# The first expert layer reordered: round 0 between the shared gate-ups, loads that wait for a gather, the shared down-projection in halves

## The reference

```python
scores = sigmoid(h @ router_w);  idx = top_k(scores + bias, 8)        # 64 experts, 8 for each token
gates  = s_sel / sum(s_sel) * 2.5
y_e    = (silu(xb @ w_gate[e]) * (xb @ w_up[e])) @ w_down[e]          # w_gate, w_up: 1024x256, w_down: 256x1024
shared = (silu(h @ sh_gate) * (h @ sh_up)) @ sh_down                  # one more expert that sees every token
x      = x + g_f * (sum over a token's experts of gate * y_e + shared)
```

## The time before, and how its profile is read

| what | value |
|---|---|
| median of three runs | 1809.76 us (1802.72, 1809.76, 1810.55) |
| the profiled execution: its own time | 1802.14 us |
| its span, first to last instruction | 1800.4 us |
| PE busy | 1642.2 us, 91% |
| DVE, ACT, POOL busy | 32%, 17%, 11% |
| data moved | 563.94 MB, mean 313 GB/s |
| mean granted TensorE clock | 0.974 |

### The profile page before, as it was taken

How to read it: one execution, slowest core, us unless ns; L and a number is a source line. 1 busy time by engine, 2 the same in 40 slices (tenths; PEclk the granted TensorE clock), 3 DMA queues, 4 the chain that set the end, 5 groups by cost and what they waited for, 6 DMA issues and landing times. The chain is left out here.

```text
span 1800.4 us, 23106 instructions
## 1 busy us (share of the span) xinstructions
PE 1642.2 (91%) x8503; PEld 725.1 (40%) x8503; DVE 580.2 (32%) x1357; ACT 298.7 (17%) x679; POOL 206.4 (11%) x197
## 2 busy tenths in 40 slices
PE   4999998999999898999998599989799899798897
PEld 2544444554333333434333244454333233233232
DVE  3131775464221122222121552375322122112122
ACT  2002443130111111111111121173100000000001
POOL 0300442001111111111110000030100000000000
PEclk9999999999999999999999799999899899999899
DMA  9613983066999999999999952303999999999995
GB/s 347 186 59 132 354 315 113 20 260 241 420 400 406 420 415 404 403 408 400 416 412 403 359 215 81 106 1 106 394 408 387 419 418 414 419 418 419 416 411 206
DMA packets 127841, 563.94 MB, mean 313 GB/s; under 512 B 17802, under 2 KB 23385, under 8 KB 78192
## 3 DMA queue, kind: packets, MB, share of 16 engines
q1 hardware_dynamic: 109344, 515.40, 71.8%
q0 software_dynamic: 17248, 43.62, 6.4%
q10 hardware_dynamic: 1136, 3.43, 0.5%
HBM read 553.10 MB, written 26.83 MB: 322 GB/s over the span
## 5 line engine op out<-in xcount | busy, mean ns | idle before, releaser
L1861 PE MATMUL ps<-wb,pool 128*32 128x512 f32 (+2 forms) x2608 | 493.0, 606 | 21.9 <-issue 21.8
L1861 PEld LDWEIGHTS ps<-wb,pool 128*32 128x32 f32 (+2 forms) x2608 | 160.2, 125 | 310.9 <-issue 310.9
L1875 DVE TENSOR_TENSOR ffn_hid<-ffn_sg,ps 128x256 f32<-128x256 f32 x71 | 29.9, 421 | 567.5 <-ACT ffn_sg L1869 567.5
L1905 PE MATMUL ps<-pool,ffn_hidT 128*32 128x512 f32 (+2 forms) x584 | 164.1, 597 | 3.5 <-DVE ffn_hidT L1890 2.3
L1905 PE MATMUL ps<-hT,ffn_hidT 128*32 128x512 f32 (+2 forms) x680 | 158.2, 603 | 5.0 <-DVE ffn_hidT L1890 3.2
L1762 POOL DMA_INDIRECT pool<-h_rows,ffn_index x71 | 73.5, 1036 | 613.6 <-DVE ffn_index L1812 318.5
L2579 PE MATMUL ps<-wb,hT 128*128 128x512 f32 x320 | 139.7, 597 | 3.0 <-issue 1.6
L1869 ACT ACTIVATE ffn_sg<-ps 128x256 f32<-128x256 f32 x71 | 27.2, 383 | 571.1 <-PE ps L1861 571.1
L1932 PE MATMUL ps<-x_res,rw 128*128 128x512 f32 x224 | 114.1, 613 | 0.9 <-DVE x_res L1944 0.9
L1905 PE MATMUL ps<-sh_wd,ffn_hidT 128*32 128x512 f32 (+2 forms) x272 | 100.1, 596 | 2.3 <-DVE ffn_hidT L1890 1.5
L1825 PE MATMUL ps<-const,pool 128*128 128x128 f32 x568 | 91.0, 284 | 10.0 <-DMA pool<-h_rows,ffn_index 7.9
(11 more groups left out here) (336 smaller groups left out, 1751.4 us busy)
## 6 DMA issues: line engine op xcount, KB each, us to landing
wb<-in_expert_w_gate_dram SPq DMA_DIRECT2D x106, 1024.0 KB, 13.1
wb<-in_expert_w_up_dram SPq DMA_DIRECT2D x106, 1024.0 KB, 19.0
pool<-in_expert_w_down_dram SPq DMA_DIRECT2D x52, 1024.0 KB, 19.9
hT<-in_expert_w_down_dram SPq DMA_DIRECT2D x52, 1024.0 KB, 17.9
wb<-in_ada_w_dram SPq DMA_DIRECT2D x24, 2048.0 KB, 10.7
sh_wd<-in_expert_w_down_dram SPq DMA_DIRECT2D x24, 1024.0 KB, 19.0
wb<-in_diff_w_in_dram SPq DMA_DIRECT2D x6, 2048.0 KB, 17.5
mix_yr<-y_rows SPq DMA_DIRECT2D x6, 2048.0 KB, 15.5
```

The lines of the kernel that those rows point to most:

```text
L1861: mm = nc.tensor.matmul(core.ps[lo:lo + width, gu_bank(n), :], xT[:, n % 2, k, lo:lo + width], w[:, k], start=k == 0, stop=k == KD - 1, sk ...
L1875: nc.vector.tensor_tensor(hid[:, n % 2, :], sg[:, n % 2, :], core.ps[:, gu_bank(n), F:2 * F], ALU.mult).then_inc(hid_ready, 1)
L1905: mm = nc.tensor.matmul(core.ps[lo:lo + width, down_bank(half), :], hidT[:, n % 2, k, lo:lo + width], wd_at(q % DR, half, k), start=k == 0 ...
```

## The change

In layer 0 only (`last` is False). The helper functions take new positions (`pos_shared`, `pos_round`), since shared tiles and rounds now share the semaphores and the two buffers of gate-up sums in the order shared 0, 1, 2, round 0, shared 3, round 1, ...

1. PE does the placing product at once and not after the second shared gate-up; the shared gate-ups 1 and 2 are cut in halves around `pe_info(0)` and `pe_turn(0)`; round 0's gate-up stands between shared gate-up 2 and 3, and `pe_info(1)` and round 0's down before round 1.
2. SP issues gate-up 0 and 1, then waits until the first gather has landed, then gate-up 2, 3, down 0, 1, gate-up 4, 5, down 2 to 5, and from 6 on gate-up q, down q. Down loads 0 to 11 use a ring of four slots, since `sh_wd` is still in use; from 12 on the ring has five.
3. The shared down-projection is cut in eight halves, each 512 columns of one tile (2 products), two in each of rounds 1 to 4, through PSUM bank 7, each followed by two DVE operations on 512 columns.
4. In every round both transposes of the next round (half 1 first) stand before `pe_turn_hidden(n)`; and for rounds from 6 on (`HEAD_ROUNDS`) one chunk of k of the next round's gate-up (`EARLY_CHUNK` = 4) stands between `pe_turn_hidden(n)` and down n. With it the wait for the next round's gate-up weights moves ahead of down n.

```diff
+        X_HALVES = (0, 1) if last else (1, 0)
+        HEAD_ROUNDS = 6
+        EARLY_CHUNK = KD // 2
+        def chunks_early(n):
+            return () if last or n < HEAD_ROUNDS else (EARLY_CHUNK,)
+        def pos_shared(i):
+            return i if last else (0, 1, 2, 4)[i]
+        def pos_round(n):
+            return n if last else 3 if n == 0 else n + 4
+        D_FOURS = 0 if last else 12
+            s = q % DR if last else q % 4 if q < D_FOURS else (q - D_FOURS - 1) % DR
...
+        def pe_shared_half(pe, j):
+            i, half = j // 2, j % 2
+            if j == 0:
+                pe.wait_ge(wd_in, 16)
+                pe.wait_ge(sums_used, 1)
+            else:
+                pe.wait_ge(sh_scaled, j)
+            pe.wait_ge(sh_hidT, pos_shared(i) + 1)
+            pe.wait_ge(index_ready, 3 if j >= 6 else 2)
+            for k in range(KF):
+                mm = nc.tensor.matmul(core.ps[:, 7, :], sh_hidden[i][:, k, :], sw.wd[:, k, half * 512:(half + 1) * 512],
+                                      start=k == 0, stop=k == KF - 1)
+            mm.then_inc(sh_down, 1)
+        def dve_shared_half(dve, j):
...
+            nc.vector.tensor_tensor(sh_prod[:, j % 2, :], core.ps[:, 7, :], r.ffn_gate[...], ALU.mult).then_inc(sh_scaled, 1)
+            dve.wait_ge(sh_scaled, j + 1)
+            nc.vector.tensor_tensor(core.x[:, t, cols], core.x[:, t, cols], sh_prod[:, j % 2, :], ALU.add).then_inc(sh_added, 1)
...
+                    for q in range(2):
+                        sp_gate_up(sp, q)
+                    sp.wait_ge(gathered[0], 16)
+                    for q in range(2, 4):
+                        sp_gate_up(sp, q)
+                    for q in range(2):
+                        sp_down(sp, q)
+                    over = overflow(sp)
+                    for q in range(4, 6):
+                        sp_gate_up(sp, q)
+                    for q in range(2, 6):
+                        sp_down(sp, q)
+                    for q in range(6, E):
+                        sp_gate_up(sp, q)
+                        if q < E - 2:
+                            sp_down(sp, q)
...
+                    dve_shared_hidden(dve, 0)
+                    dve_info(dve, 0, link)
+                    dve_shared_hidden(dve, 1)
+                    dve_shared_take(dve, 0)
...
+                    dve_take_x(dve, 0)
+                    dve_shared_take(dve, 1)
+                    dve_shared_hidden(dve, 2)
+                    dve_hidden(dve, 0)
+                    dve_hot(dve, 1)
+                    dve_shared_take(dve, 2)
+                    dve_shared_hidden(dve, 3)
+                    dve_info(dve, 1, link)
+                    dve_take_hidden(dve, 0)
+                    dve_take_x(dve, 1)
+                    dve_shared_take(dve, 3)
...
+                    pe.wait_ge(taken, 2 * NT - 1)
+                    pe_shared_gate_up(pe, 1, 0, KD // 2)
+                    pe_info(pe, 0)
+                    pe_shared_gate_up(pe, 1, KD // 2)
+                    pe_shared_turn(pe, 0)
+                    pe_shared_gate_up(pe, 2, 0, KD // 2)
+                    for half in X_HALVES:
+                        pe_turn(pe, 0, half)
+                    pe_shared_gate_up(pe, 2, KD // 2)
+                    pe_shared_turn(pe, 1)
+                    pe_gate_up(pe, 0, chunks_rest(0))
+                    pe_shared_gate_up(pe, 3)
+                    pe_shared_turn(pe, 2)
+                    pe_info(pe, 1)
+                    pe_turn_hidden(pe, 0)
+                    for half in X_HALVES:
+                        pe_turn(pe, 1, half)
+                    pe_shared_turn(pe, 3)
+                    for half in range(2):
+                        pe_down(pe, 0, half)
...
+                    pe_gate_up(pe, n, chunks_rest(n))
...
                     if n + 1 < R:
-                        pe_turn(pe, n + 1, 0)
+                        for half in X_HALVES:
+                            pe_turn(pe, n + 1, half)
                     pe_turn_hidden(pe, n)
-                    if n + 1 < R:
-                        pe_turn(pe, n + 1, 1)
+                    if n + 1 < R and chunks_early(n + 1):
+                        pe_gate_up(pe, n + 1, chunks_early(n + 1))
                     for half in range(2):
                         pe_down(pe, n, half)
+                        if n <= NT:
+                            pe_shared_half(pe, 2 * (n - 1) + half)
```

More of the change, by code:

```diff
@@ L1742, in sp_down @@
         def sp_down(sp, q):
-            if q >= DR:
-                sp.wait_ge(down1_ready, plan.last(q - DR) + 1)
+            if d_prev[q] is not None:
+                sp.wait_ge(down1_ready, plan.last(d_prev[q]) + 1)
             elif q < 2:
@@ L1787, in pe_info @@
                 pe.wait_ge(index_ready, b)
+                if not last:
+                    pe.wait_ge(sums_used, 1)
+                    if b >= 2:
+                        pe.wait_ge(sh_scaled, 6 if b == 2 else 2 * NT)
             for m, n in enumerate(plan.batch_rounds(b)):
@@ L1816, in pe_turn @@
             s = n % XS
-            if half == 0:
+            if half == X_HALVES[0]:
                 pe.wait_ge(gathered[s], 16 * (n // XS) + 16)
+                if n == 0 and not last:
+                    pe.wait_ge(g_taken, NT // 2)
             if last and half == 1:
@@ L1865, in act_silu @@
         def act_silu(act, n):
[L1866 to L1875 removed]
+            at = pos_round(n)
@@ L1895, in pe_down @@
                 for q in plan.begins(n):
-                    pe.wait_ge(d_in[q % DR], 16 * (q // DR) + 16)
-                pe.wait_ge(hidT_ready, n + 1)
+                    pe.wait_ge(d_in[d_slot[q]], 16 * d_turn[q] + 16)
+                pe.wait_ge(hidT_ready, pos_round(n) + 1)
+                if n == 0 and not last:
+                    pe.wait_ge(scratch_free, 1)
             if last and half == 1:
@@ L2143, in _ @@
                         slot = n % STREAM
-                        sp.wait_ge(gu_ready, plan.last(E - GU + (slot - E) % GU) + 1)
+                        sp.wait_ge(gu_ready, pos_round(plan.last(E - GU + (slot - E) % GU)) + 1)
                         core.stream.feed(sp, n + 1, core.stream.start["ada1_head"])
@@ L2194, in _ @@
                         act.dma_start(r.h_rows[i * P:(i + 1) * P, :], hrow[:, i, :]).then_inc(rows_out, 16)
-                for i in range(1, NT):
-                    act_shared_silu(act, i)
+                act_shared_silu(act, 1)
                 act_take_x(act, 0)
+                if not last:
+                    act_shared_silu(act, 2)
+                    act_silu(act, 0)
+                    act_shared_silu(act, 3)
+                    act_take_x(act, 1)
                 over = overflow(act)
-                for n in range(R):
+                for n in range(0 if last else 1, R):
                     if n >= 1 and not last:
@@ L2405, in _ @@
                     mm.then_inc(turned, 1)
-                pe.wait_ge(taken, 2 * NT - 1)
-                pe_shared_gate_up(pe, 1)
+                if last:
+                    pe.wait_ge(taken, 2 * NT - 1)
+                    pe_shared_gate_up(pe, 1)
                 pe.wait_ge(mask_u_ready, 1)
```

257 lines of the change are left out of this document (147 added, 110 removed).

## The result

The changed kernel takes 1817.61 us (median of 8 runs, 1814.23 to 1823.61), the kernel before on the same chip 1804.78 us (8 runs, 1800.64 to 1810.55). The ratio is 1.0068 with a 95% interval of 1.0046 to 1.0089: 12.3 us slower. That is inside the range of the prediction but not its likeliest case: the forecast was "no difference", and the time went to the side of rival B, which had a chance of 0.19. That it lies inside is in part luck: the kernel before came out 5 us lower here than the 1809.76 that the range was built on, and 1809.76 with 12.3 us more would be 1822.1, just past its end.

The account below looks back on a forecast made before the run. PE sets the pace most of the time, with the DMA engines nearly as full. Loads 0, end +3.6 and dips -2 give +1.6 us (head's 2.2 absorbed): 1809.8 + 1.6 = 1811.4 us, range 1796 to 1822.

Parts of the forecast that it names:

- rival B: Experts' rounds: the moved weight wait delays releases and starves the loads; +18 us, 1828, or +9 to +14; chance 0.19.
- The head: PE up to round 5: new waits and rounds 1 to 4 make round 5 start 2.2 us late, absorbed by round 13.
- SP's wait for the gather: SP's load queue: gate-ups 2, 3 and downs 0, 1 queue behind the gather, needed some 20 us later; hidden, no cost.
- The +0.3 us for each of rounds 1 to 4: PE's handoff without a chunk: both transposes first take 2.56 us against 2.25, +1.2 us in all.
- Earlier loads: Head's weight loads: the ring hands the earlier start back before load 11; 0, bounds 0 and 2.8 us of gain.
- DMA share well below 1 from 486 to 500 us: Sign in the changed profile: DMA engines stand idle before load 11, which goes out at 498 to 501.
- The new order within a round: Rounds with the early chunk: PE saves 0.57 us each, but weights take it; counted 0, bounds 0 and -15 us.
- Rival A: Experts' rounds: DMA engines follow a faster PE, so its saving comes through; 1788 in full, 1800 at half; chance 0.28.
- The wait that moved: Weight wait now ahead of down n: waited-for gate-ups end 3.6 us later; +3.6 at layer 0's end, bounds 0 and 3.6.
- The rate: DMA transfer rate of layer 0: earlier requests from 800 to 900 us fill one or two dips; -2 us of 10.
- The ring of four: Down loads up to 11: DMA engines lose about 1 us between loads 11 and 12; nothing on the path, bound 1 us.
- Shared down in halves: Rounds 1 to 4: waits for DVE between halves are covered by PE's work; nothing, bound 5.6 us.

Follow-up runs that it names:

- e3: Changed kernel with SP issuing down loads 2 and 3 ahead of gate-up loads 4 and 5; ratio 1.0038 to the kernel before.
- e11: Kernel before with both transposes ahead of the hidden transpose in each round and no early chunk; ratio 0.9997 to the kernel before.
- e7: Changed kernel without the early chunk and with down loads 2 and 3 ahead of gate-up loads 4 and 5; ratio 0.9998 to the kernel before.
- e10: Kernel before with both transposes first and, from round 6, the early chunk only in rounds beginning one expert; ratio 0.9998 to the kernel before.
- e8: Changed kernel with downs 2, 3 before gate-ups 4, 5, gate-up 12 before down 11, early chunk only for rounds beginning one expert; ratio 0.9997 to before.
- e12: Changed kernel with no early chunk in the last round; ratio 1.0076 to the kernel before.
- e6: Kernel before with only the new order in the rounds: both transposes first, early chunk from round 6; ratio 1.0036 to the kernel before.
- e1: Changed kernel without the early chunk in any round; ratio 1.0036 to the kernel before.
- e4: Changed kernel with down loads 2 and 3 ahead of gate-ups 4 and 5, and gate-up 12 ahead of down 11; ratio 1.0035 to the kernel before.
- e2: Changed kernel with SP issuing gate-up load 12 ahead of down load 11; ratio 1.0075 to the kernel before.
- e13: e4 with the early chunk and its weight wait moved between the two halves of the down-projection; ratio 1.0029 to the kernel before.
- e9: Changed kernel with SP's wait for the first gather taken out; ratio 1.0124 to the kernel before.

## Where the prediction was right, and where it failed

The range held, but the forecast was "no difference", built as +1.6 us from its terms with -6 to +9 around it, and +12.3 is outside that. Two terms were far too small, one had the wrong sign, and one counted a loss that was not there, which made up for some of it by luck.

**The head, +2.2 us: measured +7.0.** This is the first step that failed, and it failed in "SP's wait for the gather". I checked down 0 and 1 ("the first to be needed ... four loads at 420 GB/s are 15 us. Hidden") and stopped there. The next pair, down 2 and 3, goes out at 420.74, when `hT` is free, behind gate-ups 4 and 5. From 401.44 on the queue carries twelve loads up to and with down 3: 12.6 MB, 30 us at the 420 GB/s that I used and 36 at the 347 of the first row of after's stretches, so down 3 lands between 431.4 and 437.7. PE, now 20 us ahead in its rounds, wants it at 434.4. The same sum would have shown that the cover is gone, and e3 shows that the late landing is the cause. The terms that I did work out there were small and on the safe side: the onehot wait was 0.34 us and not 1, the gather's 0 and not 1, the waits of the two transposes 0.22 and 0.28. The +0.3 us for each of rounds 1 to 4 is not there in e11, whose rounds are 12.82 us. Without the late downs the head is 0.9 us longer than before in e7 and 1.4 in e3: these small terms, +2.2 in the prediction, were of the right order. Nor was the head's loss absorbed, as the sum has it: the 5.6 us that e3 has regained by the end of round 5's gate-up are still 5.2 at the end of round 42's (its rows in the table, 14.1 and 9.0, unrounded 14.13 and 8.97). The clock's part, 2.4 of the 7.0 us, is in no term of mine, since the kernel before had no idle stretch in which it fell.

**Earlier loads, 0: right.** e7 shows it without the two losses: gate-ups 4 and 5 go out at 424.9 and 426.8 us, where before has 433.8 and 436.8, which, counted from SP's first gate load, is 13 and 14 us sooner, and the ratio is 0.9998. The sign "DMA share well below 1 from 486 to 500 us" came out as 0.72 (0.66 in e7, 0.95 before). Load 11 went out at 506.4 and not at 498 to 501, because the head was late; with the order of e3 round 5 ends at 500.10, as foreseen.

**The new order within a round: right in its size, and right that the weights take it.** 12.82 to 12.20 is 0.6 us, and over all 37 rounds the saving is 0.55 us each, where the prediction has 0.57. The weight waits, foreseen at "20 or 27 us", are 27.6. In e10 PE waits 7.8 us longer for weights than before (17.1 for 9.3) in the same time: so much it had saved elsewhere, and "PE may gain only what the DMA engines allow". Rival A is refuted by it: the mean rate stays at 410 or 411 GB/s in e7, e8 and e10, whatever PE saves.

**The wait that moved, +3.6 us at the end: right mechanism, wrong place, wrong sum.** e12 shows that the end term is not there. I had taken the weights of round 42 as landing just when PE is through with down, as before (0.34 us of wait), and added down's 3.6 us to that. In the changed kernel they land at 984.85, and PE would want them at 988.07 (e12): the waits of the rounds before have put PE back by more than the loads, and the end has nothing left to lose. What the moved wait costs lies in the rounds before, 0.3 to 0.4% in three comparisons (e6 against before, the changed kernel against e1, e4 against e7). I had priced it "about 1 us in two places", by the shortest queues of the kernel before, and left two things out. First, the waits become longer than the 2.1 us of the earlier trace rows, up to 5.3, because a round that begins two experts needs the loads of both before its first product, and the chunk asks for them a down earlier. All thirteen weight waits are in such rounds, and e10 and e8, which leave out just those rounds, lose nothing. Second, PE works at 1.2 GHz after some of them: 9.1 us of extra time in the five rounds above. No term and no rival had the clock in it. The rounds' sum is then -20.2 (what PE saves, 0.55 us in each of 37), +18.3 (weight waits, 27.6 for 9.3) and +9.1 (clock), which is the +7.1 up to rounding. The sizes are read from the trace; no run kept the waits and the clock apart, and why the clock fell after some waits and not after longer ones is open.

**The rate, -2 us: wrong in sign.** It fell to 401 GB/s with a share of 0.99 (e6: 405). 9 GB/s over 470 us are 10 us of transfer: the idle transfer time of rival B, though the runs do not show whether it comes from the later releases or from PE being slower at the low clock. I had set a share below 0.97 as the sign of rival B, which was too coarse: 1% of 470 us is already 4.7 us, and a stall's clock shows in no share of the DMA engines at all.

**The ring of four, about 1 us and nothing on the path: not contradicted.** No ratio moves with it (e2, e4 against e3); the profiles have the rounds 1.6 and 3.1 us shorter without it, which is less than the ratios can tell.

**Shared down in halves, 0: right to 1 us.** The halves take 1.98 us, with nothing waited for. From the end of round 1's gate-up to that of round 5, e7 takes 66.5 us and before 51.2, 15.3 more, of which 14.4 are the shared downs themselves.

**What stays open.** e13 has neither long waits nor a lower clock in the rounds, and still 1.0029. Its slower rounds account for 2 us, its profile for 3.0, its ratio for 5.2 (interval 2.3 to 8.3); between the two lies no cause that I have shown. No version was clearly faster than the kernel before: e7, e8, e10 and e11 are level with it, 0.7% faster than the changed kernel.

## What to carry to other kernels

When a queue of loads is reordered, work out the landing of every load up to the point where the old order is back, each against the moment at which its consumer, itself moved, wants it; here the loads were followed up to down 1, and downs 2 and 3, with gate-ups 4 and 5 ahead of them, cost 0.3%. A wait that is moved ahead of independent work has to be priced by its longest case and with the clock after it, above all in those steps that need two transfers at once. A saving on PE is worth nothing while the weights set the pace, so the same edit is best tried first where no long wait moves with it.

## What the runs showed of the hardware

**A stall can cost more than its length.** Idle stretches of PE of 4.3 to 5.3 us between matmuls (round 1; round 8 of the changed kernel and of e6) were each followed by matmuls at 1.2 GHz: eight products in 3.68 us for 1.94, sixteen in 5.38 for 3.65. So were four shorter weight waits of the changed kernel, of 1.46, 1.98, 2.13 and 3.33 us, each at a price of 1.7 to 2.7 us, while after others of 2.03, 2.11 and 2.63 us the clock was full. Where the wait stood ahead of a whole gate-up, up to 2.3 us in e8, the granted clock of 505 to 975 us was 1.00. The page "TensorE: Matmul & The Clock Gate" of the Trainium skill, section "HAM oscillation — how this bites in real kernels", describes waits for DMA between groups of matmuls that leave each group to start at the low clock; the traces here agree for the longest waits, with single stalls in an otherwise full stream, and have both outcomes for the shorter ones.

**What the DMA engines move.** Over 470 us they moved 409 to 411 GB/s in the kernels without long waits (before, e7, e8, e10, e13), at a share of 1.00. Short stretches lie above that: 420 to 427 GB/s around the two longest waits (434 to 439 us and 531 to 537 us), and 420 over 50 us of the kernel before. A PE that waits for weights is no sign that they run full: during the waits of rounds 20, 24, 31 and 39 they moved 375, 364, 317 and 275 GB/s. The page "DMA: Bandwidth & Descriptors" of the Trainium skill, section "Bandwidth", has 425 GB/s for a 16 MB transfer; the best short stretches agree with it, the mean over 470 us does not.

**Stores and gathers among a row of loads.** The gather of 128 rows of h landed in 6.0 us on a nearly idle queue, and in 4.5 in the changed kernel, where SP holds its loads back for it. With gate-ups 2 and 3 and downs 0 and 1 (six transfers of 1 MB) issued ahead, it took 7.9 us, and the stores of its rows 12.7 for 8.8, so that PE waited 11.03 us (e9).
